# A transformer pair on one core: the second score matmuls of a grouped-attention step issued one key block later

## What is computed

```python
def block(args):
    qb, i = args                              # 128 queries
    kb = lax.dynamic_slice_in_dim(kp, start, BAND, axis=1)
    vb = lax.dynamic_slice_in_dim(vp, start, BAND, axis=1)
    ...
    s_band = jnp.einsum('bqhgd,bjhd->bhgqj', qb, kb).astype(f32) * ATTN_SCALE
    s_band = jnp.where(mask, s_band, NEG_INF)
    s_ctx = jnp.einsum('bqhgd,bjhd->bhgqj', qb, kc).astype(f32) * ATTN_SCALE
    p = sink_softmax(jnp.concatenate([s_ctx, s_band], axis=-1)).astype(vb.dtype)
    return (jnp.einsum('bhgqj,bjhd->bqhgd', p[..., :n_ctx], vc)
            + jnp.einsum('bhgqj,bjhd->bqhgd', p[..., n_ctx:], vb))
```

## Time and profile before

| | us |
|---|---|
| median of 3 runs | 1720.45 |
| lowest and highest | 1716.83, 1722.75 |
| the profiled execution | 1721.67 |
| its span in the trace | 1719.6 |
| last attention in the trace, about | 1512.6 to 1661.8 |

### The profile page before, as it was taken

How to read it: one execution, slowest core, us unless ns; L and a number is a source line. 1 busy time by engine, 2 the same in 40 slices (tenths; PEclk the granted TensorE clock), 3 DMA queues, 4 the chain that set the end, 5 groups by cost and what they waited for, 6 DMA issues and landing times.

```text
span 1719.6 us, 22679 instructions
## 1 busy us (share of the span) xinstructions
PE 1588.1 (92%) x7940; PEld 1192.6 (69%) x7940; DVE 936.6 (54%) x2204; ACT 764.2 (44%) x1411; POOL 494.5 (29%) x220
## 2 busy tenths in 40 slices
PE   7998999999899999998999999999989697979897
PEld 5885666677688888885777777677667477745455
DVE  7136555283788767556556444644471593156642
ACT  6227766524333222345335443554443531246653
POOL 4542232344244444442211111111224242310012
PEclk9999999999899999999999999999999899979999
DMA  6851112363466665431101111111111131210001
GB/s 193 175 140 45 61 57 73 115 224 115 146 196 193 197 188 195 156 98 62 50 31 44 38 37 37 37 37 37 37 38 50 37 90 59 77 34 1 1 13 62
DMA packets 48397, 149.28 MB, mean 87 GB/s; under 512 B 5782, under 2 KB 9110, under 8 KB 48184
## 3 DMA queue, kind: packets, MB, share of 16 engines
q1 hardware_dynamic: 37080, 112.45, 21.7%
q10 hardware_dynamic: 11232, 35.72, 6.4%
HBM read 141.53 MB, written 6.62 MB: 86 GB/s over the span
## 4 chain that ended last, share of the span: by engine, by line
PE 73%; DVE 14%; ACT 6%; issue 4%; DMA 1%; POOL 0%; ACTq 0%; DVEq 0%; SPq 0%
PE ps L317 37%; PE ps L321 18%; PE ps L497 3%; PE ps L1192 3%; PE ps L516 3%; PE ps L527 3%; PE ps L1228 2%; DVE b_sb L615 1%; DVE x2l L1806 1%; ACT sb L580 1%; DVE xn L1800 1%; PE ps L1204 1%; PE ps L971 1%; DVE ropea L1932 1%; ACT w_h L302 1%
## 5 line engine op out<-in xcount | busy, mean ns | idle before, releaser
L890 POOL TENSOR_TENSOR w_l<-raw,w_h 128x1024 fp32r<-128x1024 f32 (+1 forms) x190 | 457.1, 2406 | 993.8 <-ACT w_h L302 993.8
L302 ACT ACTIVATE w_h<-raw 128x1024 fp32r<-128x1024 f32 x190 | 200.8, 1058 | 396.6 <-PE ps L317 330.6
L317 PE MATMUL ps<-x2h,w_h 128*128 128x512 f32 (+1 forms) x816 | 248.5, 370 | 46.1 <-DVE x2l L1806 22.6
L317 PE MATMUL ps<-x1h,w_h 128*128 128x512 f32 x584 | 239.0, 409 | 19.9 <-POOL w_l L890 10.3
L317 PE MATMUL ps<-x2h,w_l 128*128 128x512 f32 (+1 forms) x816 | 232.0, 350 | 0.0
L321 PE MATMUL ps<-x2l,w_h 128*128 128x512 f32 (+1 forms) x816 | 231.8, 349 | 0.0
L317 PE MATMUL ps<-x1h,w_l 128*128 128x512 f32 x584 | 231.4, 396 | 0.0
L321 PE MATMUL ps<-x1l,w_h 128*128 128x512 f32 x584 | 230.8, 395 | 0.0
L317 PEld LDWEIGHTS ps<-x2h,w_h 128*128 128x128 f32 x816 | 132.3, 190 | 95.1 <-issue 56.1
L317 PEld LDWEIGHTS ps<-x2h,w_l 128*128 128x128 f32 x816 | 132.1, 191 | 20.7
L321 PEld LDWEIGHTS ps<-x2l,w_h 128*128 128x128 f32 x816 | 132.4, 191 | 19.9 <-issue 0.2
(11 more groups left out here) (310 smaller groups left out, 2490.6 us busy)
## 6 DMA issues: line engine op xcount, KB each, us to landing
raw<-in_w_mlp SPq DMA_DIRECT2D x64, 512.0 KB, 4.2
mraw<-in_w_mod ACTq DMA_DIRECT2D x51, 512.0 KB, 3.8
raw<-in_w_a SPq DMA_DIRECT2D x32, 512.0 KB, 3.5
raw<-in_w_att SPq DMA_DIRECT2D x25, 512.0 KB, 11.2
raw<-in_w_b SPq DMA_DIRECT2D x20, 512.0 KB, 3.5
raw<-in_w_g SPq DMA_DIRECT2D x16, 512.0 KB, 3.6
raw<-in_w_ao SPq DMA_DIRECT2D x9, 512.0 KB, 3.5
gates<-g_stage ACTq DMA_DIRECT2D x16, 256.0 KB, 2.1
```

The lines of the kernel that those rows point to most:

```text
L302: nc.scalar.activation(split(u)[0], raw[:, u % RAW], ACT.Copy).then_inc(w_hi, 1)
L317: mm = nc.tensor.matmul(o, w[:, k], xh(k), start=(first and k == k0 and wi == 0), stop=(last and k == k1 - 1 and wi == 1))
L890: nc.gpsimd.tensor_tensor(l[:, ks], raw[:, u % RAW, ks], h[:, ks].bitcast(F32), ALU.subtract).then_inc(w_lo, 1)
```

## The change

One number: in `attn_out` the scores of heads 2 and 3 of step n+2 are issued in the loop's pass for block 2 and no longer in that for block 1. Since `turn(b)` stands ahead of them and `weigh(b - 1)` behind them, they come behind `weigh(0)` and `turn(2)`.

```diff
             for b in range(nb):
                 turn(b)
                 A.between_pe(pe, A.blk[n] + b)
-                if A.slots == 2 and b == 1:
+                if A.slots == 2 and b == 2:
                     attn_scores(pe, A, n + 2, (2, 3))
                 if b:
                     weigh(b - 1)
```

## The result

The changed kernel takes 1748.12 us (median of 4 runs, 1746.43 to 1749.16) against 1719.94 us before (4 runs); the ratio is 1.0163, 95% interval 1.0144 to 1.0183. The forecast was 1746, and it was the case of a fallen clock that came, not rival 1 at 1737.

A forecast was written before the change was run, and what follows sets the result against it. The prediction saw no full engine in the grouped attention but a loop of hand-overs. To the profiled 1721.67 us it added 15.5 for the order (8.3 + 7.05 + 0.1) and 9 for the clock: 1746 us, range 1734 to 1754.

The forecast's parts named there:

- the case of a fallen clock: Grouped attention: the clock falls in most of six TensorE holes; 1746 us, 1741 to 1752, chance 0.62.
- rival 1: Grouped attention: the holes come but the clock stays up and they cost nothing; 1737 us, chance 0.20.
- (a): Even turns 2 to 12: the moved scores start 0.86 to 1.76 us later, behind ScalarE's first transpose copy; 8.3 us.
- (c): Turns 0 and 1: ScalarE's first transpose copy starts early in turn 1, so 0.1 us in all.
- (b): Odd turns 3 to 13: the moved scores add their own length, 1.07 or 1.28 us each; 7.05 us.
- (d): Odd turns: six TensorE holes of about 3 to 4 us lower the clock, 1.5 us each; 9 us.
- Rival 2: Moved scores' waits for DVE: the 9.7 us simply go, faster at 1712 us; chance 0.03.
- Rival 3: Attention loop: (a) or (b) is absorbed by unseen slack in the chain; 7 to 8 us, 1729 us, chance 0.05.
- Rival 4: TensorE holes: the slow clock lasts, 3 us for each hole; 1755 us, chance 0.07.

The follow-up runs named there:

- the filled kernel: Changed kernel plus 6 to 9 unused matmuls in each odd turn 3 to 13, two fewer than first filled kernel: 1735.66 us, ratio 1.0090.
- the two halves: Kernel before with the scores of heads 2 and 3 one block later only in even turns, or only in odd: 1732.54 and 1734.68 us.
- the deferred finish: Kernel before, with ScalarE's copy of a finished output behind the next exponentials and DVE's remainder one step later: 1716.44 us, ratio 0.9989.
- the even half: Kernel before with the scores of heads 2 and 3 one block later in even turns only: 1732.54 us, ratio 1.0072.
- the odd half: Kernel before with the scores of heads 2 and 3 one block later in odd turns only: 1734.68 us, ratio 1.0094.
- the first filled kernel: Changed kernel plus eight to eleven unused matmuls in each odd turn 3 to 13: 1739.63 us, ratio 1.0128.

## Why the prediction was right

**What is queued where.** That C0 stands behind the exponentials and that W0, now ahead of S23, inherits that hold was the step on which all rested. The run with C0 moved ahead of the exponentials in odd turns shows it: the loss vanishes.

**(a) Even turns**, 8.3 us. S23 stands in turns 4, 6, 8 and 12 where it was put. In turn 2 it came 0.44 us later than reckoned, in turn 10 0.24 (0.44 in the filled kernel), and 0.44 too in turn 1, for which (c) had 0.1 us in all. The place in turn 2:

```profile
1543.55 1.10 PE L516 MATMUL ps<-ident,b_sb 128*128 128x128 f32 x8 [0.54 <-DVE b_sb L650]
...
1545.34 0.65 PE L527 MATMUL ps<-b_pt,b_v 128*64 128x256 f32 x4 [0.69 <-ACT b_pt L564]
```

T0 waits for the scaled rows of its own step, since S23 of the four-block turn before came late. The prediction had no term for this wait in the sum of (a) to (c); its bound of one microsecond was for a late C0, and the order's part came 1.4 us above the sum.

**(b) Odd turns**, 7.05 us. Pairs of turns in the filled kernel against before: 4 and 5 +2.83 us (forecast 1.76 + 1.07 = 2.83), 6 and 7 +2.41 (2.42), 8 and 9 +2.31 (2.14), 2 and 3 +3.01 (2.56), 10 and 11 +3.00 (2.56), 12 to 15 +2.85 (2.83), turn 1 +0.54 (0.1). The sum is 16.95 against 15.5. The even and the odd turns stand in pairs here, so these figures show the sum of (a) and (b) in each pair, not each alone.

**(d) The clock.** Six falls behind six holes, of 2.95 to 3.99 us, as forecast. The size was low: 11.7 us instead of 9, 1.95 a fall instead of 1.5, because two of the slow stretches lasted 6.8 us. Laid turn by turn against the second filled kernel, from W0 to the start of the next turn, the four falls of 3.4 us cost 1.6 us each, as priced, and the two long ones (turns 5 and 11) 2.9 each. S23 of turn 9 takes 2.50 us in a slow stretch, where a wide one has 1.35 in the earlier trace rows:

```profile
1623.77 2.50 PE L497 MATMUL ps<-b_k,b_q 64*128 64x256 f32 x8
1626.20 0.85 PE L527 MATMUL ps<-b_pt,b_v 128*64 128x256 f32 x4
```

So the 28.6 us in the trace are 16.9 + 11.7 where 15.5 + 9 were forecast. The time is 2 us above 1746, which looks better than the forecast was: the loss is 28.2 us where 24.5 were forecast, and 1.7 us of the difference were made up by luck, since the sum started from a profiled execution of 1721.67 us and the median before is 1719.94.

**The rivals.** Rival 1 is what the filled kernel measures: 1735.7 us against the 1737 worked out for it, so the order's part was priced nearly rightly (16.3 us against 15.5), but its condition (the clock stays up) did not hold. Rival 2 fell by the row it named: W0 of turn 6 waits 0.65 us behind T1, where the prediction found it short by 0.6. Rival 3 fell with the two halves, each of which is over 13 us slower, and with the pairs of turns above, which leave no part absorbed. Rival 4 took 3 us a hole; two of the six cost 2.9 us each, the other four half as much.

## What to carry to other kernels

Before work is put into a wait, see what that work is itself waiting for: the engine that feeds it may have its piece in a queue behind something longer, and then the wait is only exchanged. What is moved back must be followed to everything that starts from it; here the eight matmuls that lost 1.3 us started a chain of 9.6 us over two other engines. And where such a loop leaves holes on TensorE, price the clock too: it was 12 of the 28 us behind holes of 3 to 4 us, and single falls came behind holes of 1.5 to 2.4 us as well.

## What the runs showed of the hardware

- The same idle 1.71 us on PE at the same place was followed by a full clock in one kernel and by a fall in another (the deferred finish). In the even half 1.51 us were followed by a fall in turn 13 and by none in turn 5; in the odd half 1.78 us by a fall in turn 5 and 2.69 us by none in turn 7. Whether a hole of this length brings a fall can't be read off the hole alone.
- At full clock a matmul of 256 f32 columns took 0.43 us with a stationary operand of 128 columns (the extra ones of the first filled kernel), and two with 64 columns each, the weighted sums of one key block, took 0.58 us together (1593.26 to 1593.84 in the earlier trace rows).
- Useless matmuls that fill a hole can pay for themselves: 12 us here (28.2 us of loss without them, 16.3 with them).
